# Reordering the stage seams of an eight-stage fp32 transformer kernel

## The reference

```
mod = c_act @ ada_w[l] + ada_b[l]
sh_m, sc_m, gt_m, sh_f, sc_f, gt_f = split(mod, 6)
h = rms_norm(x, norm_mix[l]) * (1 + sc_m) + sh_m
x = x + gt_m * mixer(h)
h = rms_norm(x, norm_ffn[l]) * (1 + sc_f) + sh_f
g, u = split(h @ w_in);  x = x + gt_f * ((silu(g) * u) @ w_out)
```

## Time and profile before

| | us |
|---|---|
| Median of 3 runs | 2988.85 (2986.52 to 2989.19) |
| The profiled execution | 2986.99 |
| its span | 2985.2 |
| PE busy (95% of the span) | 2838.4 |
| DVE, ACT, POOL busy | 1426.2, 969.1, 560.2 |
| granted TensorE clock, mean | 0.981 of full |

### The profile page before, as it was taken

How to read it: one execution, slowest core, us unless ns; L and a number is a source line. 1 busy time by engine, 2 the same in 40 slices (tenths; PEclk the granted TensorE clock), 3 DMA queues, 4 the chain that set the end, 5 groups by cost and what they waited for, 6 DMA issues and landing times.

```text
span 2985.2 us, 32393 instructions
## 1 busy us (share of the span) xinstructions
PE 2838.4 (95%) x13466; PEld 2289.6 (77%) x13466; DVE 1426.2 (48%) x2082; ACT 969.1 (32%) x1300; POOL 560.2 (19%) x441
## 2 busy tenths in 40 slices
PE   6979989899999999999999999899999998999998
PEld 4758677688887878877888887578888875788886
DVE  5463464767546333345232444645445455444353
ACT  3353343322224321234222333432222334322222
POOL 3444351110112211221101200012112100021121
PEclk9999989999999999999999999999999999999999
DMA  6311111446423222222532322122222321122321
GB/s 237 112 42 64 59 48 59 181 161 228 182 78 110 89 74 85 89 71 90 153 132 81 104 101 70 53 71 95 94 101 84 114 69 64 59 99 78 113 81 67
DMA packets 49810, 294.30 MB, mean 99 GB/s; under 512 B 6345, under 2 KB 6473, under 8 KB 23808
## 3 DMA queue, kind: packets, MB, share of 16 engines
q1 hardware_dynamic: 43632, 274.48, 26.0%
q0 software_dynamic: 4736, 15.43, 2.0%
q10 hardware_dynamic: 1296, 2.32, 0.2%
HBM read 283.56 MB, written 8.65 MB: 98 GB/s over the span
## 4 chain that ended last, share of the span: by engine, by line
PE 87%; DVE 7%; ACT 4%; issue 1%; POOL 1%; DMA 0%; SPq 0%; DVEq 0%; ACTq 0%
PE ps L218 86%; DVE wlo L211 1%; PE ps L1294 1%; ACT whi L200 0%; DVE F L2219 0%; DVE F L409 0%; DVE hl L413 0%; DMA F<-in_ada 0%; ACT F L1311 0%; ACT F L1270 0%; ACT hh L427 0%; DVE E L2780 0%; DVE ada L457 0%; DVE F L1261 0%; DVE ada L364 0%
## 5 line engine op out<-in xcount | busy, mean ns | idle before, releaser
L218 PE MATMUL ps<-hh,whi 128*128 128x512 f32 x2088 | 830.8, 398 | 21.7 <-DVE wlo L211 7.5
L218 PE MATMUL ps<-hl,whi 128*128 128x512 f32 x2088 | 818.7, 392 | 0.0
L218 PE MATMUL ps<-hh,wlo 128*128 128x512 f32 x2088 | 817.9, 392 | 0.0
L211 DVE TENSOR_TENSOR wlo<-raw,whi 128x2048 fp32r<-128x2048 f32 (+2 forms) x235 | 495.8, 2110 | 538.7 <-ACT whi L200 538.6
L218 PE MATMUL ps<-R,whi 128*128 128x512 f32 x2080 | 649.5, 391 | 7.8 <-DVE wlo L211 2.8
L200 ACT ACTIVATE whi<-raw 128x2048 fp32r<-128x2048 f32 (+2 forms) x235 | 409.6, 1743 | 693.5 <-PE ps L218 693.5
L218 PEld LDWEIGHTS ps<-hh,whi 128*128 128x128 f32 x2088 | 395.8, 190 | 116.7 <-issue 8.9
L218 PEld LDWEIGHTS ps<-R,whi 128*128 128x128 f32 x2080 | 390.4, 188 | 94.8 <-issue 6.9
L218 PEld LDWEIGHTS ps<-hl,whi 128*128 128x128 f32 x2088 | 395.0, 189 | 84.2
L218 PEld LDWEIGHTS ps<-hh,wlo 128*128 128x128 f32 x2088 | 395.9, 190 | 82.6 <-issue 2.4
L218 PE MATMUL ps<-R,wlo 128*128 128x512 f32 x1040 | 404.7, 389 | 0.0
(11 more groups left out here) (335 smaller groups left out, 2644.5 us busy)
## 6 DMA issues: line engine op xcount, KB each, us to landing
F<-in_ada SPq DMA_DIRECT2D x32, 1024.0 KB, 4.8
raw<-in_fs0in SPq DMA_DIRECT2D x22, 1024.0 KB, 5.7
raw<-in_fs1in SPq DMA_DIRECT2D x22, 1024.0 KB, 4.8
raw<-in_fc0in SPq DMA_DIRECT2D x22, 1024.0 KB, 4.8
raw<-in_fc1in SPq DMA_DIRECT2D x22, 1024.0 KB, 4.8
Rf<-in_ada0h SPq DMA_DIRECT2D x24, 512.0 KB, 3.5
raw<-in_fs0out SPq DMA_DIRECT2D x16, 704.0 KB, 4.4
raw<-in_fs1out SPq DMA_DIRECT2D x16, 704.0 KB, 4.2
```

Of the source, the lines that this page charges most:

```text
L211: e.tensor_tensor(m.wlo[n % 2][:, 0:size], m.raw[m.slot[n]][:, 0:size], m.whi[n % 2][:, 0:size].bitcast(F32), SUB).then_inc(*s.up("wlo", n))
L218: return e.matmul(out, l, r, start=start, stop=stop, skip_group_check=True)
```

## The change

Five edits. (1) Chain i is done by DVE one slab later (at slab i+1), its sum taken by PE at slab i+2, and SP issues the piece for it one slab later. (2) `act_rs` loads the table before it waits for the squares. (3) In the last output slab of the two mixers that end in a modulated seam, DVE does the shift sums and the next slab's `wlo` before the two low parts `hl` of the previous slab's chunks. (4) `dve_norm` has six places instead of four at the three seams. (5) Unit 0's two products are taken out of PSUM (`dve_first_unit`) right after the norm, ahead of chain 0 and of `wlo` of the third slab, and PE's third slab waits for that alone.

```
 def act_rs(e, s, m, st, bank):
+    table(e, s, ACT.Ln)
     s.wait_ge("squares", st)
...
+def norm_slot(m, gain, n):
+    return m.f(m.FN - T * (n % NORM_SLOTS[gain] + 1))
...
             # dve_norm
-            if n >= 4:
-                s.wait_ge("h_hi", gain, n - 4)
-                if (n - 4) % 2:
-                    s.wait_ge("h_lo_pool", gain, n - 4)
+            if n >= 6:
+                s.wait_ge("h_lo_pool" if n % 2 else "h_hi", gain, n - 6)
...
+NORM_SLOTS = {"nm0": 4, "nf0": 6, "nm1": 6, "nf1": 6}
...
             # pe_ffn
-            if u >= 2:
+            if prev and u == 2:
+                s.wait_ge("first_up", st)
+            elif u >= 2:
                 s.wait_ge("gate_g" if conv else "gate", st, u - 2)
                 s.wait_ge("gated", st, u - 2)
...
             # dve_ffn, slab 0
                 dve_slab(e, s, m, n + 1)
                 dve_norm(e, s, m, {"s0": "hyb", "s1": "ret"}[st])
-                dve_ffn_ada(e, s, m, st, n)
+                dve_first_unit(e, s, m, st, n)
...
+def dve_first_unit(e, s, m, st, n):
+    s.wait_ge("tile", n, "all")
+    for bank, at, signal in ((0, T1, "first_gate"), (1, T2, "first_up")):
+        e.tensor_tensor(m.f(at), m.ps[bank][:, :], m.rs[:, :], MUL).then_inc(*s.up(signal, st))
...
             # dve_ffn_unit, u == 0
-        s.wait_ge("tile", n, 0)
-        s.wait_ge("rs", {"s0": "hyb", "s1": "ret"}[st])
-        e.tensor_tensor(a, m.ps[0][:, :], m.rs[:, :], MUL).then_inc(*s.up("first_gate", st))
-        s.wait_ge("tile", n, "all")
-        e.tensor_tensor(out, m.ps[1][:, :], m.rs[:, :], MUL).then_inc(*s.up("first_up", st))
...
             # sp_ffn
-            for k in ((0, 1, 2) if i == 0 else (i + 2,)):
+            for k in ((0, 1, 2) if i == 0 else (i + 1,) if i > 1 else ()):
...
             # dve_ffn_ada
-    i = n - m.at["fs0in", 0]
-    if st != "s0":
+    i = n - m.at["fs0in", 0] - 1
+    if st != "s0" or i < 0:
         return
...
             # pe_ffn_ada
-    i = n - m.at["fs0in", 0] - 1
+    i = n - m.at["fs0in", 0] - 2
...
             # dve_mix_out
         dve_slab(e, s, m, n + 1)
+        if st in MODULATED and not half and j == 3:
+            dve_x(e, s, m, st, 2 * j - 2)
+            dve_x(e, s, m, st, 2 * j - 1)
         for c in range(2):
             dve_residual(...)
-        if not half:
+        if not half and not (st in MODULATED and j == 2):
             dve_x(e, s, m, st, 2 * j)
             dve_x(e, s, m, st, 2 * j + 1)
```

More of the change, by code:

```diff
@@ L398, in dve_norm @@
     at, c = MOD[gain], m.acol[:, 8:10]
-    slot = lambda n: m.f(m.FN - T * (n % 4 + 1))
+    slot = lambda n: norm_slot(m, gain, n)
     s.wait_ge("ada_sum", "shift", st)
@@ L420, in act_norm @@
     for n in range(8):
-        a, hi, b = m.f(m.FN - T * (n % 4 + 1)), m.h(n)[0], m.mod[:, at + n:at + n + 1]
+        a, hi, b = norm_slot(m, gain, n), m.h(n)[0], m.mod[:, at + n:at + n + 1]
         s.wait_ge("normed", gain, n)
@@ L434, in pool_norm @@
     for n in range(1, 8, 2):
-        a, (hi, lo) = m.f(m.FN - T * (n % 4 + 1)), m.h(n)
+        a, (hi, lo) = norm_slot(m, gain, n), m.h(n)
         s.wait_ge("h_sum", gain, n)
@@ L538, in act_start_norm @@
     for n in (2 * i, 2 * i + 1):
-        a, hi, b = m.f(m.FN - T * (n % 4 + 1)), m.h(n)[0], m.mod[:, n:n + 1]
+        a, hi, b = norm_slot(m, "nm0", n), m.h(n)[0], m.mod[:, n:n + 1]
         s.wait_ge("normed", "nm0", n)
@@ L563, in dve_start_norm @@
 def dve_start_norm(e, s, m, i):
-    slot = lambda n: m.f(m.FN - T * (n % 4 + 1))
+    slot = lambda n: norm_slot(m, "nm0", n)
     at, a = 2 * i, m.acol[:, 2 * i:2 * i + 2]
```

## The result

The changed kernel takes **2967.05 us** (median of 4 runs, 2965.01 to 2967.95) against 2987.97 for the kernel before measured beside it: ratio 0.9929, 95% interval 0.9912 to 0.9946. That is 20.9 us less. The forecast was 2966.4, with a range of 2961 to 2974, and "faster by over 0.2%" at 0.92.

A forecast was written before the change was run, and what follows sets the result against it. PE's work, 95% of the span, was taken as the bound, so only its waits and slow matmuls could be won. Terms 3.4 + 10.8 + 4.2 + 2.85 + 1.2 = 22.5 us gave 2966.4 us, range 2961 to 2974.

The forecast's parts named there:

- Term 1: Seams into FFN s0 and s1: shift sums ahead of the low parts remove PE's first-slab wait, 3.4 us for both.
- Term 2: Second slab of FFN s0: chain one slab later gains 12.8 us, a new third-slab wait gives back 2.0; net 10.8.
- rival A: Third slab of s0: POOL holds up the products, wait 3.1 us, and the clock falls; 2.6 worse, 2969 us; 17%.
- Term 3: Third slab of FFN s1: earlier product and table load remove the wait and the slow matmuls behind it, 4.2 us.
- Term 4: Retention's first scores: table loaded ahead cuts the 2.59 us wait to 1.3, and 1.57 of slow matmuls goes; 2.85 us.
- Term 5: Program's end: the last table load fills ACT's idle time before `rs`, 1.2 us gained.
- the six places: DVE's norms at the three seams: six places instead of four gain nothing, since DVE never waits for a place.

The follow-up runs named there:

- the undone part: Changed kernel with one edit reversed: under Term 1 shift sums behind the low parts again, median 2967.87 us; under Term 2 chains one slab earlier again, 2979.46.
- the plain wait: Six idle DVE instructions ahead of `wlo` of s0's third slab, added to the changed kernel with chains one slab later still; one run, 2969.37 us.
- the kernel with the old order: Changed kernel with DVE making the two `hl` before the shift sums again at the mixers' last slab; median 2967.87 us, against 2965.15 for the control.
- the copies: The changed kernel itself, unaltered, measured again as control beside other kernels; medians 2965.15 and 2969.60 us.

## Why the prediction was right

**The bound** was read rightly: the change wins only what PE waits and what it runs slowly after a wait. The spans differ by 19.1, the span less PE busy by 19.3; that PE busy changed by only 0.2 is in part luck, since the hybrid stage took back what the seams gained at the clock.

**Term 1 (3.4)**: 3.7 by the undone part. The bound on what POOL could cost the sums (3.0 in all) covered what it did cost, 2.0.

**Term 2 (10.8)**: 10.0 by the undone part, or 9.2 without that execution's longer slow stretch; and the first seam's own jumps give 11.46 - 0.50 - 1.7 (term 1) = 9.3. So the term was 1.5 too large. The failed step is "I take no fall, because the one-column matmuls cut the wait in two". The fall, which is rival A's second half, came and cost 1.5. Idle times of 1.43 (the plain wait) and of 1.81 to 1.84 (before the scores, eight traces of nine) kept the clock, and 1.69 with the one-column matmuls in the gap lost it in seven traces of seven: they didn't rescue it, and probably lengthen the gap. The idle time was 1.69 for 2.0, but PE's next full matmul was late by 2.49, 0.8 more than the idle time, where the sum had 0.43 for the one-column matmuls; that takes back the 0.3. Rival A's first half, products held up by POOL, didn't happen. The Trainium skill ("SBUF — State Buffer", section "Who interferes with whom") says that a DVE instruction with at most one SBUF input, outside the two-port modes, does not contend with GpSimd. The traces agree for the products, which took 1.27 beside POOL, and from the other side: the shift sums, with two SBUF inputs, go from 3.61 to 5.58 beside POOL, and POOL's L1186 from 1.29 to 3.25 beside `wlo`. One SBUF input alone isn't enough, though: the TENSOR_SCALAR of the earlier trace rows has one too and took 1.41 beside POOL for 0.34. In which mode it ran no trace shows.

**Term 3 (4.2)**: the seam as a whole gained 6.02, of which term 1 has 1.75, so 4.3. The parts undone singly give only 1.50 and 0.57. The old wait of 2.48 was the product path (1.24) and the table (1.28) end to end, so with either edit undone only a short wait comes back (1.24 or 0.28), and behind neither does the clock fall (the first matmul takes 0.47 in both). The clock's 1.57 is thus won by either edit, and the term can't be split between them.

**Term 4 (2.85)**: 2.74. The wait was 1.81 and not 1.3, since PE reaches the scores 0.5 earlier itself, a wait of 0.22 for `wlo` at the value slab having gone. The 1.57 for the clock went as hoped, but in part by luck: with this wait one trace in nine shows the fall.

**Term 5 (1.2)** and **the six places (0)** came out to the tenth.

**The sum**: 22.5 forecast, 20.9 at the seams; the missing 1.6 is term 2, by the size of the fall of the clock. In the total this can't be seen, since executions of one program differ by more; that 2966.4 came within 0.7 of the median is partly luck.

## What to carry to other kernels

Where one engine is 95% busy, list its waits, follow each to the instruction that releases it, and price a reorder by what becomes last there next, the slower matmuls behind a wait included. Don't count on small matmuls in a wait to keep the clock up: in seven traces of seven here they didn't. When single executions differ by more than the parts of a change, compare the starts of a repeated instruction in two traces: the jumps show each part to some tenths of a us.

## What the hardware showed unexpectedly

- PE at its lower level (1.2 of 2.4 GHz) after short waits isn't a matter of the wait alone. At the seams, by how late PE's next full matmul started: after 1.4 us (the products undone, s1), 1.58 (the plain wait) and 1.59 it held; after 2.0 at the scores it held in eight traces (4.58 us for the sixteen) and fell in one (6.28); after 2.49 with one-column matmuls in between it fell in all seven traces that have it, and so it did after 4.5 with them in it (the products undone, s0). In one of the seven, the kernel with the old order, PE first ran five matmuls at full speed and slowed 1.2 us after the wait. Why it fell once in nine at the scores stays open; no kernel was made that shifts only the time at which a wait falls. PE's timeline of the old order:

```profile
563.52 0.39 PE L218 MATMUL ps<-hh,wlo 128*128 128x512 f32 x1
563.75 0.52 PE L218 MATMUL ps<-hl,whi 128*128 128x512 f32 x1
564.07 0.63 PE L218 MATMUL ps<-hh,whi 128*128 128x512 f32 x1
```

- The slow stretch is seven to eleven matmuls long behind waits at the same place. The Trainium skill ("TensorE: Matmul & The Clock Gate", section "Part 1: The HAM clock gate") says that the number of slow matmuls at a kernel's start varies from run to run; the traces show the same behind a wait: seven before and eleven with the chains back, both after 10.7 us. Whether the copies' 1.00 against 0.83 in the hybrid stage has the same cause no run shows.
- DVE and POOL hold each other up, in both directions: 2.28 us of `wlo` on DVE made a POOL addition that started after it 1.96 us longer, nearly by its whole length, and where the addition started 0.5 ahead of `wlo`, it stayed at 1.29 and `wlo` grew by 0.66, to 2.94.
